# Two transformer blocks at 256 tokens on one core: where the tensors lie in SBUF

## What is computed

```python
for layer in range(DEPTH):                      # first block
    h = h + gla_mixer(...)  or  h + diff_mixer(...)
    h = h + sqrelu_mlp(rms_norm(h, mlp_norm[layer]), mlp_w1[layer], mlp_w2[layer])
u = rms_norm_2(h, norm_mix)                     # second block
proj = u @ w_in
merged = gates_0 * y_conv + gates_1 * y_ssd + gates_2 * y_window_attention
h = h + merged @ w_mix_out
h = h + memory_cross_attention(...)
h = h + jnp.square(jax.nn.relu(rms_norm_2(h, norm_mlp) @ w_mlp_up)) @ w_mlp_down
```

## The kernel before

| tensor | address before | mod 1024 | address in the changed order | mod 1024 |
|---|---|---|---|---|
| `raw` | 16512 | 128 | 32768 | 0 |
| `w_hi` | 49280 | 128 | 65536 | 0 |
| `w_lo` | 65664 | 128 | 81920 | 0 |
| `H` (residual) | 73856 | 128 | 90112 | 0 |
| `par` | 82048 | 128 | 8320 | 128 |
| `con` | 89184 | 96 | 15456 | 96 |
| `arena` (everything else) | 104256 | 832 | 98304 | 0 |
| `xa_both`, `xa_bf` | 186176, 202560 | 832 | 180224, 196608 | 0 |
| `xb_both`, `xb_bf` | 206656, 223040 | 832 | 200704, 217088 | 0 |
| `rstd` | 97984 | 704 | 24160 | 608 |
| `small_hi` | 227136 | 832 | 30304 | 608 |

## Time and profile before

### The profile page before, as it was taken

The page is one execution under the profiler, slowest core; times in us unless marked ns, Lnnn a source line. Parts: engine busy times, 40 slices in busy tenths (PEclk is TensorE's granted clock), DMA queues, the critical chain, the costliest instruction groups (busy, mean ns, idle before and its releaser), DMA issues. The chain is left out here.

```text
span 1598.9 us, 26385 instructions
## 1 busy us (share of the span) xinstructions
PE 1437.6 (90%) x9598; PEld 1180.1 (74%) x9622; DVE 1059.0 (66%) x1664; ACT 883.2 (55%) x1702; POOL 440.5 (28%) x437
## 2 busy tenths in 40 slices
PE   5996999999988999989888779898898989799998
PEld 5885877768767777769877667777777779587775
DVE  4794766666655766646999745667576666376664
ACT  4433645456556554447988655454565466454453
POOL 3000632343003433324887100003000003073322
PEclk9997999998987999989999989999999989999999
DMA  7230555553822555534343322224434335145551
GB/s 299 106 129 3 185 189 202 187 185 113 204 80 82 193 198 186 184 132 159 132 158 141 123 87 101 103 106 156 140 127 142 129 129 187 41 181 195 187 202 59
DMA packets 35305, 233.55 MB, mean 146 GB/s; under 512 B 3840, under 2 KB 6912, under 8 KB 7936
## 3 DMA queue, kind: packets, MB, share of 16 engines
q1 hardware_dynamic: 30816, 223.75, 38.3%
q10 hardware_dynamic: 3216, 4.19, 1.7%
q0 software_dynamic: 1168, 4.20, 0.9%
HBM read 227.93 MB, written 4.19 MB: 145 GB/s over the span
## 5 line engine op out<-in xcount | busy, mean ns | idle before, releaser
L1515 DVE TENSOR_TENSOR w_lo<-raw,w_hi 128x1024 bf16<-128x1024 f32 x420 | 539.6, 1287 | 233.5 <-ACT w_hi L960 229.4
L960 ACT CAST w_hi<-raw 128x1024 fp32r<-128x1024 f32 x420 | 437.5, 1045 | 266.9 <-PE ps L389 113.3
L383 PE MATMUL ps<-xa_both,w_hi 128*128 128x256 f32 x1040 | 273.7, 302 | 31.0 <-ACT w_hi L960 11.8
L384 PE MATMUL ps<-xa_both,w_hi 128*128 128x256 f32 x1040 | 257.2, 286 | 0.0
L383 PEld LDWEIGHTS ps<-xa_both,w_hi 128*128 128x128 f32 x1040 | 204.9, 197 | 40.5 <-issue 16.3
L384 PEld LDWEIGHTS ps<-xa_both,w_hi 128*128 128x128 f32 x1040 | 205.3, 197 | 0.5
L423 PE MATMUL ps<-xa_both,w_hi 128*128 128x512 f32 x768 | 204.7, 407 | 0.1
L442 PE MATMUL ps<-w_hi,xb_both 128*128 128x512 f32 x384 | 167.1, 435 | 0.0
L2141 POOL TENSOR_SCALAR arena<-arena 128x256 f32<-128x256 f32 x96 | 86.6, 902 | 284.8 <-DVE arena L1583 284.8
L383 PE MATMUL ps<-xb_both,w_hi 128*128 128x256 f32 x576 | 149.8, 299 | 13.6 <-DVE xb_both L1528 7.9
L389 PE MATMUL ps<-xa_bf,w_lo 128*128 128x256 bf16 x1040 | 141.3, 281 | 21.5 <-DVE w_lo L1515 21.5
(11 more groups left out here) (294 smaller groups left out, 2351.3 us busy)
## 6 DMA issues: line engine op xcount, KB each, us to landing
raw<-weights SPq DMA_DIRECT2D x210, 1024.0 KB, 4.8
band<-arena ACTq DMA_DIRECT2D x1, 3072.0 KB, 36.5
arena<-band POOLq DMA_DIRECT2D x8, 256.0 KB, 3.2
arena<-gla_masks SPq DMA_DIRECT2D x1, 1088.0 KB, 15.1
H<-x_t SPq DMA_DIRECT2D x1, 1024.0 KB, 5.1
arena<-mem_t POOLq DMA_DIRECT2D x1, 1024.0 KB, 5.3
arena<-band POOLq DMA_DIRECT2D x8, 128.0 KB, 2.8
out_t<-H ACTq DMA_DIRECT2D x8, 128.0 KB, 2.1
```

The lines of the kernel that those rows point to most:

```text
L383: mm(ps[:, bank, 0:T], w_hi[:, s, k], X.hi[:, k], start=k == 0, stop=False)
L384: mm(ps[:, bank, 0:T], w_hi[:, s, k], X.lo[:, k], start=False, stop=False)
L960: nc.scalar.copy(w_hi[:, j % HI_SLOTS].rearrange("p k n -> p (k n)"), raw[:, j // 2 % RING, j % 2]).then_inc(hi_done, 1)
L1515: TT(w_lo[:, j % HI_SLOTS].rearrange("p k n -> p (k n)"), raw[:, j // 2 % RING, j % 2], w_hi[:, j % HI_SLOTS].rearrange("p k n -> p (k n)" ...
```

## The change

The small tensors are asked for first and the large ones last. `small_hi` and `small_lo`, which stood behind everything, move to the front too. A filler of 176 float32 values, used by nothing, makes `raw` start at 32768. The scratch for GpSimd's transfers becomes 8192 bytes. No instruction is added, removed or moved; only addresses differ.

```diff
-        raw = sb("raw", [P, RING, 2, D])
-        w_hi = sb("w_hi", [P, HI_SLOTS, KC, P], F32R)
-        w_lo = sb("w_lo", [P, HI_SLOTS, KC, P], BF16)
-        H = sb("H", [P, KC, T])
         par = sb("par", [P, NPAR])
         con = sb("con", [P, NCON])
...
+        small_hi, small_lo = sb("small_hi", [P, KC * SSD_HEADS], F32R), sb("small_lo", [P, KC * SSD_HEADS], BF16)
...
         gains = sb("gains", [P, 8])
+        sb("fill_up", [P, 176])
+        raw = sb("raw", [P, RING, 2, D])
+        w_hi = sb("w_hi", [P, HI_SLOTS, KC, P], F32R)
+        w_lo = sb("w_lo", [P, HI_SLOTS, KC, P], BF16)
+        H = sb("H", [P, KC, T])
         ARENA = 20480
         arena = sb("arena", [P, ARENA])
...
-    nc = bacc.Bacc("TRN2", target_bir_lowering=False, num_devices=1)
+    nc = bacc.Bacc("TRN2", target_bir_lowering=False, num_devices=1, dynamic_dma_scratch_size=8192)
```

More of the change, by code:

```diff
@@ L128, in program @@
         later_b = sb("later_b", [P, P], BF16)
-        eps = sb("eps", [P, 1])
-        one = sb("one", [P, 1])
         sumsq = sb("sumsq", [P, T])
@@ L133, in program @@
         lnt = sb("lnt", [P, 2, T])
-        lnt_tok = sb("lnt_tok", [P, NT])
         rstd = sb("rstd", [P, T])
         rstd_mem = sb("rstd_mem", [P, T])
+        hn_sqb = sb("hn_sqb", [P, 2, T])
+        hn_rb = sb("hn_rb", [P, 2, T])
+        small_hi, small_lo = sb("small_hi", [P, KC * SSD_HEADS], F32R), sb("small_lo", [P, KC * SSD_HEADS], BF16)
+        eps = sb("eps", [P, 1])
+        one = sb("one", [P, 1])
+        lnt_tok = sb("lnt_tok", [P, NT])
         rtok = sb("rtok", [P, NT])
@@ L139, in program @@
         rtok2 = sb("rtok2", [P, NT])
-        hn_sqb = sb("hn_sqb", [P, 2, T])
-        hn_rb = sb("hn_rb", [P, 2, T])
         gains = sb("gains", [P, 8])
+        sb("fill_up", [P, 176])
[3 more added lines that the diff above has]
+        H = sb("H", [P, KC, T])
         ARENA = 20480
@@ L199, in program @@
         g_z = cut(T, rows=GLA_RANK + 1 + 15)
-        small_hi, small_lo = sb("small_hi", [P, KC * SSD_HEADS], F32R), sb("small_lo", [P, KC * SSD_HEADS], BF16)
         z_hi, z_lo = small_hi[:, 0:Z_COLS], small_lo[:, 0:Z_COLS]
```

## The result

| | before | after |
|---|---|---|
| median, 11 runs of each side by side | 1598.18 us (1594.31 to 1602.72) | 1605.47 us (1604.12 to 1606.74) |
| ratio after / before, 95% interval | | 1.0043 [1.0032, 1.0054] |
| profiled execution, span | 1598.9 us | 1602.5 us |
| TensorE busy with matmuls | 1437.6 us | 1445.4 us |

The changed kernel is 7.3 us slower by the medians, 0.43% by the ratio. That is inside the forecast's range and under the 0.5% that the prediction took as its bound, but it is beyond the interval of this comparison, and each run of after was longer than each of before. So "addresses don't matter" was wrong, and there is something to explain.

A forecast was written before the change was run, and what follows sets the result against it. The prediction took TensorE to bound the kernel, most fully in the MLPs. Its terms, 0 + 0 + 0 + 0 for pace, VectorE and ScalarE, transfers and scratch, left the median's 1596.5 us, range 1574 to 1612.

The forecast's parts named there:

- addresses don't matter: Whole kernel: the forecast itself, no effect beyond a few ns here and there, 1592 to 1601 us, chance 0.61.
- What bounds the kernel: Whole span: TensorE busy for 90%, 97 to 100% in the MLPs; VectorE leads in the convolution's stretch, 800 to 900 us.
- Matmul pace: TensorE's float32r matmuls: distance between starts unchanged, 0 us taken, range 40 us faster to 20 us slower.
- The page's rule: SBUF, engines' side: TensorE and ScalarE never wait on anyone, so pace cannot depend on where two tensors lie; sum 0.
- Rival 3: TensorE's matmuls: equal phases of loaded and moved streams put every form on the slow side; 20 us, 1617, chance 0.13.
- Rival 2: TensorE's matmuls: float32r's excess comes from starting points and aligned streams lose it; 8 to 40 us faster, chance 0.24.
- VectorE and ScalarE: Instruction lengths on these two engines: no effect of start addresses, 0 us taken; at most 10 us of ScalarE's work.
- Transfers: Slab loads and the start's loads: 0 us taken, with 0.3 us either way; waits are 17 us in all.
- The smaller scratch: GpSimd's 17 transfers, 16 of them bias transfers: cost 0; 51 us at stake if their cover were gone.
- Rival 4: Tensor placement: an address isn't where it was put and large tensors share another common offset; 1596 us, chance 0.02.
- The base of the sum: Starting time of the forecast: the median of the runs, 1596.5 us, with the profiled execution of 1600.8 us 4.3 above it.

The follow-up runs named there:

- e_shift128: The changed kernel with a filler of 208 instead of 176 values, all large tensors 128 bytes further, distances kept: 1605.31 us, ratio 1.0043 to the kernel before.
- e_before64: The kernel before with a filler of 64 bytes ahead of the operand sets, nothing else: 1604.59 us against 1599.55, ratio 1.0041.
- e_scratch: The kernel before with only the scratch made 8192 bytes, all distances between tensors kept: 1598.30 us against 1600.15, ratio 1.0002.

## Why the prediction was wrong, point by point

**What bounds the kernel** was right: TensorE leads, and what lengthens its matmuls goes into the time, but only where no other engine holds it. The prediction named the convolution's stretch as the exception; the ordinary chunks of XA showed that the exception is larger, as at full clock they passed on 35 to 38 of the 73 ns by which their floor rose.

**Matmul pace: the step that failed.** The prediction took 0 for this term; it is +14.4 us by cadence if nothing covered it, of which 6.2 us are found in the chunks at full clock and 4.2 in the span apart from the clock. The working had the right bounds and the right view. It saw that ordinary and token chunks, and up and down chunks, differ by what is loaded and what moves, and that this excess was the only thing an address could change. Three sentences went wrong after that:

- "The floor of the excess looks independent of the start modulo 1024": it compared the moving operand's absolute start, 832 against 128. e_shift128, and the shifts on TensorE alone, show that no absolute start matters; what the two forms differed in was the distance from the loaded to the moved operand, 192 in ordinary and up chunks and 64 in token and down chunks.
- "Every large tensor starts on a multiple of 64 bytes before as after, so an access no wider than that sees no difference": the period is 256 bytes, and 64 of them (e_before64) make the whole difference.
- "I take 0, as the value ... that needs no luck": the table of addresses held the fact that both distances went from 704 or 192 to 0. A term with a mechanism on one side and none in the middle should not have been put in the middle.

**The page's rule.** The rule cited, the Trainium skill, page "SBUF — State Buffer", section "SBUF: two separate sides", has TensorE waiting for no one. As to the other engines nothing here speaks against it, since TensorE alone reproduces the steps. Read as "TensorE's pace doesn't depend on where its tensors lie", as the prediction read it, it doesn't hold: the measurement decides, 115.1 against 119.2 ns.

**Rival 3 had the mechanism, and the wrong size.** It put the pace down to where the loaded weights and the moved columns lie relative to one another, and e_before64 and the measurements on TensorE alone confirm that. They don't confirm that equal phases are the worst case: up chunks went the other way, 233.3 to 230.9, and ordinary chunks are as slow at 72 and 96 (120.1 and 119.6) as at 0. It foretold 0.118 or more in ordinary chunks (0.1192) and 0.235 or more in down chunks (0.2315). Its 20 us counted 768 x 0.007 + 3232 x 0.0046 as if all of it lay on the path. Measured, the ordinary chunks' 0.0041 to 0.0047 a step was right, the down chunks' was 0.0016 and not 0.007, the up chunks gave 0.0024 back, and of the 14.4 us that remain less than half reached the end. The right 0.0046 was luck: it came from one token and one ordinary chunk. By the means over all chunks the two placements of before are only 0.0024 apart there, and 0.0034 instead of 0.007 between up and down chunks. The time, 1605.5 us, lies just past this rival's deciding point of 1604.

**Rival 2**, that aligned streams lose float32r's excess, falls: the bf16 step is 109.2 and 215.8 as before, and no distance tried brought float32r there.

**VectorE and ScalarE**: right. L961 has 1046 ns (1047), L1516 1225 (1226), L1222 491 to 515 (492 to 516).

**Transfers**: right. The weights' wait is 1.5 us as before, the start's wait for `par` 5.8 us (6.0).

**The smaller scratch**: right, shown by e_scratch at 1.0002; the bias transfers land after 3.1 us (3.2).

**Rival 4**, an address that isn't where it was put, has nothing for it: after, e_shift128 and e_before64 were placed by the same reckoning, the last from the old order, and their steps agree to 0.1 ns.

**The base of the sum**: the median of three runs, 1596.5, was 1.7 us below the median of eleven. That is 1.7 of the 8.9 us by which the forecast missed. And the clock, which the prediction had "no reason to expect from addresses" to change, is good for about 2.1 us more.

## What to carry to other kernels

Where a float32r matmul's pace sets the time, look at the distance modulo 256 bytes between the tensor that is loaded and the tensor that moves, for each form of product on its own, and not at the alignment of each: a filler of 64 bytes cost 0.4% here, and one of 192 bytes gave it back. Round addresses are no goal; they make distances equal by accident. And before a slower or faster step is priced by its count, ask for every group whether its chunks run at their floor, since between 4 and 6 of the 14.4 us counted here reached the end as pace; gains of 3 us and less vanished here beside changes of the granted clock. And read the pace from the mean over all chunks, not from one: single stretches made the differences between forms twice as large as they are.

## What the hardware showed that was not expected

- TensorE's float32r step depends on where its two operands lie relative to each other: 114 to 121 ns with 256 columns, 227 to 235 with 512, with a period of 256 bytes, with no other engine running. In bf16 it doesn't (109 to 110, 215 to 216). Nor does it at a granted clock of 0.5, where an ordinary float32r step takes 213 ns at either distance, like a bf16 one.
- The best distance isn't the same for two forms that read the same tensors: at 0 up chunks have their better step (230.8) and ordinary chunks nearly their worst (119.2); at 192 it is the other way round (233.4 and 115.4). Of the distances in the table, counted from the loaded to the moved operand, 192 is the lowest for 256 columns and 64 for 512, whichever of the two tensors is loaded.
- By span x clock, a layout that is 4.2 us longer in work lost 2.1 us more to the low clock, and two layouts that were 3.0 and 1.7 us shorter in work lost 2.5 and 5.0 us more. The low clock's share isn't a constant of a kernel, even where the instructions are the same.
